# Moving the row factor of a gated product from VectorE to ScalarE

## The reference, cut to what matters

```
D_FF = ((8 * D_MODEL // 3 + 255) // 256) * 256        # 5632 for D_MODEL = 2048
y = _rms(h, norm_ffn_g[i])
h = h + (jax.nn.silu(y @ w_gate[i]) * (y @ w_up[i])) @ w_down[i]
```

## Time and profile before

| | us |
|---|---|
| median of 3 runs | 1395.29 |
| profiled execution, its own time | 1396.01 |
| span of that execution, first to last instruction | 1394.3 |
| PE busy | 1385.0 (99% of the span) |
| DVE busy | 1146.4 (82%) |
| ACT busy | 788.3 (57%) |

### The profile page before, as it was taken

The page is one execution under the profiler, slowest core; times in us unless marked ns, Lnnn a source line. Parts: engine busy times, 40 slices in busy tenths (PEclk is TensorE's granted clock), DMA queues, the critical chain, the costliest instruction groups (busy, mean ns, idle before and its releaser), DMA issues.

```text
span 1394.3 us, 16628 instructions
## 1 busy us (share of the span) xinstructions
PE 1385.0 (99%) x6239; PEld 1133.1 (81%) x6239; DVE 1146.4 (82%) x1355; ACT 788.3 (57%) x1074; POOL 79.5 (6%) x64
## 2 busy tenths in 40 slices
PE   9999999999999999999999999999999999999998
PEld 7888888888888888888888888888878887777886
DVE  6589976767999988999998889977677669887796
ACT  7476755554565544565555455555465556675453
POOL 2000010000000000000000000000000144420000
PEclk9999999999999999999999999999999999999999
DMA  9766656774775746675685655686877678889654
GB/s 334 246 208 212 206 169 204 257 245 133 263 247 191 234 170 224 232 243 194 212 269 185 226 211 196 212 296 208 284 249 278 220 260 258 268 260 298 193 187 151
DMA packets 171753, 318.32 MB, mean 228 GB/s; under 512 B 11953, under 2 KB 35757, under 8 KB 171544
## 3 DMA queue, kind: packets, MB, share of 16 engines
q1 hardware_dynamic: 156792, 285.37, 61.9%
q10 hardware_dynamic: 13088, 25.18, 5.8%
q0 software_dynamic: 1792, 6.71, 1.5%
HBM read 293.04 MB, written 24.17 MB: 228 GB/s over the span
## 4 chain that ended last, share of the span: by engine, by line
PE 90%; DVE 6%; DMA 2%; ACT 1%; issue 1%; SPq 0%; POOL 0%; ACTq 0%; DVEq 0%; POOLq 0%
PE acc L1924 15%; PE acc L1926 14%; PE acc L1925 14%; PE acc L2110 12%; PE acc L2113 12%; PE acc L2112 12%; DVE w_lo L1198 3%; PE acc L1986 1%; PE tp L2110 1%; PE tp L2113 1%; PE tp L2112 1%; PE sp L2113 1%; PE sp L2112 1%; PE sp L2110 1%; DMA parked<-tile 1%; PE sp L2214 1%
## 5 line engine op out<-in xcount | busy, mean ns | idle before, releaser
L795 ACT ACTIVATE w_hi<-w_raw 128x1024 fp32r<-128x1024 f32 x541 | 564.8, 1058 | 462.1 <-PE acc L1926 229.2
L1198 DVE TENSOR_TENSOR w_lo<-w_raw,w_hi 128x1024 fp32r<-128x1024 f32 x530 | 639.8, 1226 | 175.6 <-ACT w_hi L795 171.2
L1924 PE MATMUL acc<-w_lo,hh 128*128 128x512 f32 x528 | 207.9, 394 | 0.0
L1926 PE MATMUL acc<-w_hi,hl 128*128 128x512 f32 x528 | 205.7, 390 | 0.0
L1925 PE MATMUL acc<-w_hi,hh 128*128 128x512 f32 x528 | 205.6, 389 | 0.0
L2110 PE MATMUL acc<-w_lo,yh 128*128 128x512 f32 x460 | 179.7, 391 | 0.6 <-DVE w_lo L1198 0.6
L2112 PE MATMUL acc<-w_hi,yh 128*128 128x512 f32 x460 | 179.0, 389 | 0.0
L2113 PE MATMUL acc<-w_hi,yl 128*128 128x512 f32 x460 | 179.0, 389 | 0.0
L1924 PE MATMUL acc<-w_lo,yh 128*128 128x512 f32 x416 | 162.4, 390 | 1.1 <-DVE w_lo L1198 1.1
L1926 PE MATMUL acc<-w_hi,yl 128*128 128x512 f32 x416 | 161.9, 389 | 0.0
L1925 PE MATMUL acc<-w_hi,yh 128*128 128x512 f32 x416 | 161.9, 389 | 0.0
(11 more groups left out here) (277 smaller groups left out, 1756.1 us busy)
## 6 DMA issues: line engine op xcount, KB each, us to landing
w_raw<-in_w_gate SPq DMA_DIRECT2D x88, 512.0 KB, 5.5
w_raw<-in_w_up SPq DMA_DIRECT2D x88, 512.0 KB, 6.5
w_raw<-in_w_down SPq DMA_DIRECT2D x88, 512.0 KB, 5.9
w_raw<-in_w_in SPq DMA_DIRECT2D x64, 512.0 KB, 4.6
w_raw<-in_swa_w_in ACTq DMA_DIRECT2D x48, 512.0 KB, 5.2
w_raw<-in_w_out SPq DMA_DIRECT2D x32, 512.0 KB, 5.0
w_raw<-in_w_ple_gate SPq DMA_DIRECT2D x32, 512.0 KB, 6.1
w_raw<-in_swa_w_out SPq DMA_DIRECT2D x32, 512.0 KB, 5.8
```

The source lines that it names most:

```text
L795: act.activation(w_hi[:, v % SPL], w_raw[:, s % RAW], ACT.Copy).then_inc(hi_ready, 1)
L1198: dve.tensor_tensor(w_lo[:, v % SPL], w_raw[:, s % RAW], w_hi[:, v % SPL].bitcast(F32), ALU.subtract).then_inc(lo_ready, 1)
L1924: pe.matmul(dst, xh[:, f, tk], w_lo[:, v % SPL, k], start=(f == 0), stop=False)
L1926: last = pe.matmul(dst, xl[:, f, tk], w_hi[:, v % SPL, k], start=False, stop=(f == CK * n - 1))
```

## The change

ACT does two more instructions for each of the pairs 1 to 10: after silu it multiplies each half of the gate by the row factor, in place. Each of them waits for its half of the silu by a new semaphore, `silu_part`. `silu_done` is signalled behind the second. DVE then needs no row factor, and multiplies up by gate in one instruction over 1024 columns instead of two over 512. Pair 0 has its own code and is left as it was.

```diff
                 act.wait_ge(gate_sum, m)
                 for t in range(T):
-                    last = act.activation(tok(0)[:, t], tok(0)[:, t], ACT.Silu, scale=rf[:, t:t + 1])
+                    act.activation(tok(0)[:, t], tok(0)[:, t], ACT.Silu, scale=rf[:, t:t + 1]).then_inc(silu_part, 1)
+                for t in range(T):
+                    act.wait_ge(silu_part, 2 * m - 1 + t)
+                    last = act.activation(tok(0)[:, t], tok(0)[:, t], ACT.Copy, scale=rf[:, t:t + 1])
                 last.then_inc(silu_done, 1)
...
-                b, up = PAIR[m], tok(1)
+                b = PAIR[m]
...
                 dve.wait_ge(silu_done, m)
-                for t in range(T):
-                    last = dve.scalar_tensor_tensor(up[:, t], up[:, t], rf[:, t:t + 1], tok(0)[:, t], ALU.mult, ALU.mult)
-                last.then_inc(up_sum, 1)
+                dve.tensor_tensor(gates[:, 2:4], gates[:, 2:4], gates[:, 0:2], ALU.mult).then_inc(up_sum, 1)
```

More of the change, by code:

```diff
@@ L413, in build @@
         silu_done = sem("silu_done")
+        silu_part = sem("silu_part")
         up_sum = sem("up_sum")
```

## The result

The changed kernel takes **1400.70 us** (median of 6 runs, 1400.48 to 1401.79) against 1395.92 for the kernel before (6 runs, 1394.99 to 1397.29). The ratio is 1.0035 with a 95% interval of 1.0022 to 1.0048: 4.8 us slower, and by the interval 3.1 to 6.7. The forecast was 1399.1, the range 1396.4 to 1401.2.

The account below looks back on a forecast made before the run. PE was taken to bound the kernel, without spare time behind DVE at pairs 1 and 5. 2.08 (pairs 1, 5) + 1.46 (4, 8) + 0.23 (9) = 3.77 us on 1395.29 gave 1399.1; range 1396.4 to 1401.2.

Parts of the forecast that it names:

- What bounds the kernel: PE, busy 1385.0 of 1394.3 us; at pairs 1 and 5 it has no spare time behind DVE's run.
- Two more instructions on ACT: Behind silu on ACT: the two multiplications hold ACT for 1.24 us, bounds 0.94 and 1.53; their waits cost nothing.
- the waits stop the overlap: Rival on ACT: waits hold back the next instruction, next split 1.53 us later; 1400.9 us in all, chance 0.12.
- One product instead of two on DVE: DVE's product at each pair: 1.22 us instead of 1.42, saving 0.20 behind the point where DVE lost 1.24.
- DVE's relief decides: Rival, pairs 1 and 5: ACT's extra is covered and PE gains 0.20 twice; 1394.9 us, not slower, chance 0.06.
- the rule of the Trainium skill: Relieve first the engine occupied most; between DVE's 82% and ACT's 57% it favours the change, giving 1394.9 us.
- Pairs 4 and 8: The block's own last chunk, behind silu: PE starts it 0.73 us later at each pair, 1.46 for both.
- pair 9: Low split of 885.60: 0.84 us before PE takes it, 0.03 needed; a delay of 1.04 leaves a loss of 0.23.
- Pairs 2, 3, 6, 7 and 10: First splits after these pairs: the delay is covered before PE takes the chunk, so the loss is nothing.
- the delay is swallowed: Rival: multiplication nearer the 0.47 copy, DVE fills the delay with other work; 0.9 us slower, 1396.2, chance 0.17.

Follow-up runs that it names:

- DVE's part alone: Against the kernel before: one product of 1024 columns on DVE, no multiplication on ACT, up's row factor left out; 1395.98 us against 1396.44, ratio 0.9998.
- doubled multiplications: The change plus two more multiplications on ACT by a column of ones, each with its wait; 1411.87 us against 1396.63 for the kernel before, ratio 1.0103.

## Why the prediction was right

*What bounds the kernel* held. At pairs 1 and 5 nothing lay between ACT's split and PE's chunk: counted from PE, DVE's run started 1.32 and 1.16 later, and less 0.2 this came out as 1.10 and 0.97 on PE, where 1.04 each was the step. The two lie on either side of it because, against the trace before, ACT's weights landed 0.09 later at pair 1 and 0.14 earlier at pair 5; that this nearly cancels in the sum is luck. Moving the multiplications by three splits took the whole loss away.

*Two more instructions on ACT* were sized at 1.24 from the silu rows and measured 1.23. DVE stood idle for 1.24 in front of its first split of pairs 2, 6 and 10, as was said. The Trainium skill (ScalarE: Activation LUTs, What ACT_TABLE_LOAD costs) has the same speed for every function, which made 1.22; the measured row agrees, and here it shows it for the plain multiplication, which no row of before could. That the new waits cost nothing is shown too: the first rival, "the waits stop the overlap", asked for 1.53.

*One product instead of two on DVE* was sized at 0.20 and measured 0.19 at pair 1. It comes out on PE only where DVE sets the end, by some 0.2 at pairs 1 and 5 (table above); over the stretch DVE's part alone won 0.07, as later weights took the rest. The rival "DVE's relief decides" is out. With it goes, for this kernel, the rule of the Trainium skill that stood beside it as the prediction applied it between DVE and ACT (Perfetto Trace Analysis, Identifying the Most-Contended Engine): here two more instructions a pair on the engine at 57% cost 4.5 us by their place in the order, and relieving the one at 82% won nothing that the time shows.

*Pairs 4 and 8* and *pair 9* went as worked out, as far as the wait alone goes: 0.75 for 0.73 at pair 4, 0.22 for 0.23 at the chunk of 887.66. *Pairs 2, 3, 6, 7 and 10* were to cost nothing; the change at these alone is within 0.1 us of the kernel before as a time, and 0.26 in its stretch.

**The term that was mis-sized** is what a stop of PE costs. The sum took PE's loss as the length of its wait. The trace adds 0.11 for each stop that was not there before: at pairs 3, 4, 7, 8 and 9, 0.55 in all, most of the 0.67 between 3.77 and 4.44 (at pairs 3 and 7, 0.04 of it or less is a wait). At pairs 1 and 5 it doesn't count, since the stop at 395.66 stood there before as well, and since a stop within the stretch is swallowed by the wait at its end. At pairs 3 and 7 the sum left 0.1 us to spare. PE does take pair 3's chunk on time (462.47, 0.24 behind the matmul before), and yet this matmul is shown with 0.47 and the next starts 0.31 behind it.

*The rival "the delay is swallowed"* (1396.2) fell to the same rows. The median of the changed kernel lies 4.8 over the kernel before; of the 0.3 beyond the stretch's 4.47, 0.23 is at the DMA round trip in the profiled execution, and whether the change has a part in it is open: it lies within what that place varies. And of the 1.6 between the forecast of 1399.1 and the measured 1400.70, 0.63 is the base alone: the kernel before has a median of 1395.92 over its six runs, where the forecast stood on 1395.29 from three.

## What to carry to other kernels

Before work is moved from a busy engine to an idle one, look in the timeline for what stands behind it in the idle engine's order, and how far ahead of its reader that is: here 0.03 us of spare time at one place decided, not 25 points of occupancy. Idle time in front of an instruction is no room for work behind it. If the moved work must be done, put it behind the instructions that others wait for, where the engine would wait in any case: the same two multiplications three splits later cost nothing.

## What the runs showed of the hardware

**A stop of TensorE costs more than its wait.** Behind each stop the first matmul of 512 columns is shown with 0.47 to 0.50 us and the next starts 0.31 to 0.34 behind it, where 0.39 and 0.23 are usual: 0.08 to 0.11 us for each stop of the pairs, however short it was, and even where the chunk was ready only just in time (pair 3).

**A longer stop can cost clock, and need not.** In the trace with the doubled multiplications PE waits 1.77 us for its chunk at pair 8, goes on at the usual distance for 1.3 us, and then starts a matmul every 0.43:

```profile
848.15 0.50 PE L2122 MATMUL acc<-w_lo,yh 128*128 128x512 f32 x1 [1.77 <-DVE w_lo L1212]
...
849.88 0.63 PE L2122 MATMUL acc<-w_lo,yh 128*128 128x512 f32 x1
850.30 0.63 PE L2124 MATMUL acc<-w_hi,yh 128*128 128x512 f32 x1
```

The stretches of that trace around it (window, sum of its length; busy time of PE, PEld, DVE, ACT, POOL; granted clock; DMA share and GB/s) show the granted clock at 0.55 of full speed between 849 and 852.5, that is mostly at its lower level, 1.2 GHz:

```profile
845.00:849.00 4.00, 2.23 (x10) 1.50 (x10) 2.13 (x2) 4.00 (x6) 0.00 (x0) 1.00 0.45 166
849.00:852.50 3.50, 3.50 (x11) 2.73 (x10) 2.50 (x3) 0.68 (x1) 0.00 (x0) 0.55 0.82 256
```

Eight matmuls lose 0.2 each there, 1.6 us. Of the +16.2 in the stretch of the pairs 14.6 are left, within the 14 to 15 that was expected. Four of the five timed runs show a mean granted clock of 0.997 or 0.998 and took 1411.27 to 1413.09; the one at 1.000 took 1409.81. But the same trace has a stop of the same length at pair 4, and behind that one the clock does not fall (the stretch as far behind the stop as the one above):

```profile
590.77 0.50 PE L2122 MATMUL acc<-w_lo,yh 128*128 128x512 f32 x1 [1.79 <-DVE w_lo L1212]
```

```profile
591.62:595.12 3.50, 3.50 (x17) 2.87 (x16) 3.50 (x4) 1.31 (x2) 0.00 (x0) 1.00 0.86 288
```

So the length of the stop alone doesn't decide, and what does is open. In the change itself, whose longest new waits are 0.59 us, the granted clock is 1.00 over the 4 us behind each of them. The page can't show such a fall: its slices are 35 us long, and it has nines throughout for the doubled kernel too.

**What varies most from run to run lies outside the pairs.** The kernel before ran between 1394.7 and 1400.4 over all these runs. Within the pairs the landing of weights moves DVE's run by up to 0.3 us (table above). Outside, three places move. PE comes to pair 1 between 336.02 and 337.07, whatever was changed behind it. Around 1140 us three of the traces lose 0.4 to 0.8 us. And at the end of the down projection a tile is parked in DRAM and read back. In the chain, before and after:

```profile
977.17 9.09 DMA parked<-tile
987.60 2.83 DMA tile<-parked
997.96 4.52 DMA parked<-tile
1003.81 6.41 DMA tile<-parked
```

```profile
981.59 9.00 DMA parked<-tile
991.92 2.82 DMA tile<-parked
1002.27 5.40 DMA parked<-tile
1009.01 5.86 DMA tile<-parked
```

The profiled execution with the change at pairs 2, 3, 6, 7 and 10 was the longest of its runs (1400.22, where its median is 1396.34). There the first trip took 9.70 and 4.30, PE stopped for 0.94 us at 999.21, where it doesn't stop before, and for 2.19 us (1.07 before) for a chunk behind the second trip that it took at 1018.00, and its granted clock was 0.50 from 1019 to 1022:

```profile
977.45 9.70 DMA parked<-tile
...
988.49 4.30 DMA tile<-parked
```

```profile
1019.00:1022.00 3.00, 3.00 (x8) 2.32 (x8) 2.35 (x3) 0.00 (x0) 0.00 (x0) 0.50 0.88 276
```

Its stretch of the pairs is only 0.26 longer than that of before. That is why the experiments are read there as well as by their times: an effect of 0.3 us shows in the stretch and is lost in the time.
